# Gate rows summed in the norm transitions, modulation units as halves of wider ones, and VectorE's order changed at three places

## The reference, cut to what matters

```python
mod_lat = jnp.split(jax.nn.silu(c) @ w_ada[l] + b_ada[l], 6, axis=-1)       # first block
x = x + gt2[:, None, :] * swiglu(modulate(rmsnorm(x, g_ffn[l]), sh2, sc2), w_ffn_in[l], w_ffn_out[l])

(sh1, sc1, g1, sh2, sc2, g2, sh3, sc3, g3) = jnp.split(c_act @ w_ada[l] + b_ada[l], 9, axis=-1)  # second
x = x + 0.5 * g1[:, None, :] * swiglu_2(modulate_2(rmsnorm_2(x, ffn1_norm[l]), sh1, sc1), ...)
x = x + g2[:, None, :] * (merged @ w_out[l])        # merged: two gated attention branches
x = x + 0.5 * g3[:, None, :] * swiglu_2(modulate_2(rmsnorm_2(x, ffn2_norm[l]), sh3, sc3), ...)

def swiglu_2(h, w_in, w_out):
    g, u = jnp.split(h @ w_in, 2, axis=-1)          # w_in: 1024 x 5632, w_out: 2816 x 1024
    return (jax.nn.silu(g) * u) @ w_out
```

## Time and profile before

| what | value |
|---|---|
| three runs | 1147.42 us median (1146.41 to 1147.8) |
| the profiled execution | 1146.86 us, of which the span of its instructions is 1145.1 us |
| mean granted TensorE clock | 0.992 |
| TensorE busy | 97% of the span |
| VectorE busy | 75% |
| ScalarE busy | 50% |
| HBM traffic | 218 GB/s over the span |

### The profile page before, as it was taken

The page is one execution under the profiler, slowest core; times in us unless marked ns, Lnnn a source line. Parts: engine busy times, 40 slices in busy tenths (PEclk is TensorE's granted clock), DMA queues, the critical chain, the costliest instruction groups (busy, mean ns, idle before and its releaser), DMA issues.

```text
span 1145.1 us, 19091 instructions
## 1 busy us (share of the span) xinstructions
PE 1107.0 (97%) x7728; PEld 1000.4 (87%) x7728; DVE 854.3 (75%) x1084; ACT 571.4 (50%) x733; POOL 74.8 (7%) x143
## 2 busy tenths in 40 slices
PE   2999999999999999999999999999999999999996
PEld 2899989999999888888788888889999998888885
DVE  1578795997777787777888877878677877655676
ACT  2495443544433644544554445455655646454442
POOL 4000000100001000000300000021000001000001
PEclk8899999999999999999999999999999999999999
DMA  9934656788866587778378777748865645655771
GB/s 283 302 114 135 196 159 206 215 291 267 288 212 204 173 270 255 256 258 294 107 258 291 233 249 259 234 138 267 281 203 179 229 151 184 202 185 203 233 240 37
DMA packets 192548, 250.29 MB, mean 219 GB/s; under 512 B 4859, under 2 KB 171966, under 8 KB 192350
## 3 DMA queue, kind: packets, MB, share of 16 engines
q1 hardware_dynamic: 183838, 216.92, 58.4%
q0 software_dynamic: 8640, 32.38, 8.6%
HBM read 248.23 MB, written 1.05 MB: 218 GB/s over the span
## 4 chain that ended last, share of the span: by engine, by line
PE 85%; DVE 7%; ACT 2%; SPq 2%; issue 1%; DMA 1%; POOL 0%; POOLq 0%; DVEq 0%; ACTq 0%
PE twin L1303 83%; DVE wlo L1917 2%; DVE arena L1925 2%; DVE arena L1917 1%; ACT arena L877 1%; DMA arena<-in_w_ada 1%; ACT whi L877 1%; DVE X L1917 1%; PE twin L1633 1%; SPq L574 0%; SPq L524 0%; DVE arena L1921 0%; PE twin L1754 0%; PE twin L1428 0%; DVE B_lo L1917 0%
## 5 line engine op out<-in xcount | busy, mean ns | idle before, releaser
L1303 PE MATMUL twin<-A_both,whi 128*128 128x256 f32 (+1 forms) x2208 | 577.4, 338 | 3.1 <-DVE A_both L1917 1.6
L1917 DVE TENSOR_TENSOR wlo<-raw,whi 128x2048 fp32r<-128x2048 f32 (+1 forms) x171 | 387.0, 2264 | 120.3 <-ACT whi L877 120.2
L1303 PE MATMUL twin<-A_both,wlo 128*128 128x256 f32 x1632 | 436.5, 280 | 0.0
L877 ACT ACTIVATE whi<-raw 128x2048 fp32r<-128x2048 f32 x169 | 323.2, 1912 | 198.7 <-PE twin L1303 194.9
L1303 PEld LDWEIGHTS twin<-A_both,whi 128*128 128x128 f32 x2208 | 370.1, 190 | 44.1 <-issue 6.2
L1303 PEld LDWEIGHTS twin<-A_both,wlo 128*128 128x128 f32 x1632 | 309.2, 189 | 11.4 <-DVE A_both L1917 0.6
L1925 DVE SCALAR_TENSOR_TENSOR arena<-ada_raw,arena 128x256 f32<-128x256 f32 (+2 forms) x322 | 167.3, 520 | 16.0 <-issue 1.8
L877 ACT ACTIVATE arena<-twin 128x512 f32<-128x512 f32 (+5 forms) x171 | 90.8, 556 | 116.9 <-PE twin L1303 86.3
L877 ACT ACTIVATE arena<-arena 128x512 f32<-128x512 f32 (+7 forms) x132 | 69.6, 558 | 148.8 <-DVE arena L1917 115.8
L1303 PE MATMUL twin<-whi,B_hi 128*128 128x512 f32 (+2 forms) x340 | 126.6, 372 | 0.2 <-DVE B_lo L1917 0.2
L1303 PE MATMUL twin<-wlo,B_hi 128*128 128x512 f32 (+2 forms) x340 | 125.1, 368 | 0.0
(11 more groups left out here) (137 smaller groups left out, 884.3 us busy)
## 6 DMA issues: line engine op xcount, KB each, us to landing
raw<-in_w_in SPq DMA_DIRECT2D x48, 1024.0 KB, 6.3
raw<-in_ffn_w_in SPq DMA_DIRECT2D x44, 1024.0 KB, 5.1
ada_raw<-in_w_ada POOLq DMA_DIRECT2D x28, 1024.0 KB, 6.3
ada_raw<-in_w_ada SPq DMA_DIRECT2D x24, 1024.0 KB, 5.4
raw<-in_w_ffn_in SPq DMA_DIRECT2D x22, 1024.0 KB, 5.2
raw<-in_ffn_w_out SPq DMA_DIRECT2D x22, 1024.0 KB, 5.0
raw<-in_w_ffn_out SPq DMA_DIRECT2D x11, 1024.0 KB, 5.0
arena<-in_w_ada SPq DMA_DIRECT2D x8, 1024.0 KB, 12.0
```

Source lines behind the costliest of these rows:

```text
L877: return nc.scalar.activation(o, i, f, **kw)
L1303: return nc.tensor.matmul(o, l, r, start=start, stop=stop, **kw)
L1917: return nc.vector.tensor_tensor(o, x, y, op)
```

## The change

Seven edits:

- **Cut of the modulation.** All units are now loaded and accumulated as `adapt_half` was: 512 columns by half of the rows, four VectorE instructions of 128x512 in place of eight of 128x256.
- **Counts.** The first two feed-forward blocks take 12 units each (before 10), the third none (before 4). The units are no longer at one place of each step: `ADA_STEP` = 1, 3, 6, 8, 11, 13, 16, 18, 21, 23, 26, 28, where 3i is the place after `low`, 3i + 1 after `split(u0 + 4)`, and 3i + 2 after `split(u0 + 5)` of step i. SP's queue issues the next unit right after the place of the one before.
- **Steps written out.** VectorE's and SP's steps of the feed-forward blocks are written out in place of a loop; TensorE and ScalarE loop in all three blocks.
- **Gates.** The two matmuls of a gate are split (`gate_half`). For gates 1 to 4 the first stands after the sums of shift and scale in `norm(2)` to `norm(5)`, the second after the transposes, in place of the `keep_warm` there; only `norm(3)` keeps a `keep_warm`, of 8 in place of 16. Gate 0 stands after the transposes of the last `ga` unit. Banks are chosen anew and TensorE gets waits for them (`x_piece`, `x_ready`).
- **Gate rows.** VectorE's `gate_row` of gates 1, 2 and 4 stands at the start of the feed-forward block, ahead of `split(u0 + 2)`, that of gate 3 at the start of the second mixer. TensorE waits for it (`gr_done`) in the middle of the second `up` unit, and ahead of `uq` in the second mixer. The wait for the bias moves from TensorE to VectorE.
- **End of a feed-forward block.** ScalarE's `high` and VectorE's `low` stand ahead of the `split(u0 + 3 * NF)` that they followed.
- **Second mixer.** The `split` of the second `out2` unit followed the first `brb` unit on VectorE, ahead of the low halves of the merged branches; it now follows the second `brb` unit. On ScalarE it follows the high halves in place of preceding them.

Constants and banks:

```diff
-NADA1, NADAF, NADA2 = 16, 10, 12
+NADA1, NADAF, NADA2 = 16, 12, 12
 ADA_P2 = NADA1 + 2 * NADAF
-ADA_LAST = ADA_P2 + NADA2
+ADA_STEP = [1 + 5 * j // 2 for j in range(NADAF)]
...
-            return 7 if n in (3, 4) else 3
+            return 7 if n == 4 else 0
...
-            return {0: 6, 3: 2}.get(r, 4)
+            return ((2, 3), (3, 4), (7, 3), (1, 3), (3, 5))[r][x]
```

SP's queue:

```diff
-                def step(i, m):
...
+                def next_ada(q):
+
+                    if f < 2 and q in ADA_STEP[:-1]:
+                        load_ada(NADA1 + NADAF * f + ADA_STEP.index(q) + 1)
+
+                def step(i):
+                    cs = slice(UC * i + UC, UC * i + 2 * UC)
+                    load(u0 + 2, i, w_in[:, :, cs], KD)
+                    next_ada(3 * i - 4)
+                    load(u0 + 3, i, w_in[:, :, DFF + UC * i + UC:DFF + UC * i + 2 * UC], KD)
+                    next_ada(3 * i - 3)
+                    load(u0 + 4, i, w_out[:, 2 * i:2 * i + 2, :], 2)
+                    if f < 2 and i == 0:
+                        load_ada(NADA1 + NADAF * f)
+                    next_ada(3 * i - 2)
```

ScalarE:

```diff
                 silu(NF - 1, u0, 4)
+                high(NF - 1, NF - 1)
                 split(u0 + 3 * NF)
-                high(NF - 1, NF - 1)
                 split(u0 + 3 * NF + 1)
...
                 for n2 in range(N2):
-                    if P2[n2 - 1] == ("brb", 0):
-                        split(BASE_P2 + n2 + 2)
                     if n2:
                         evac2(n2 - 1)
-                    if P2[n2 - 1] != ("brb", 0):
-                        split(BASE_P2 + n2 + 2)
+                    split(BASE_P2 + n2 + 2)
```

TensorE:

```diff
             def norm(n):
                 src = norm_source(n)
+                r = n - 1
+                if n == 3:
+                    pe.wait_ge(x_piece, 1)
                 shift_and_scale(n, column_bank(n))
-                warm = {2: 4, 5: 5}.get(n, 3)
+                if n == 4:
+                    pe.wait_ge(x_piece, 6)
+                gate_half(r, 0)
+                if n == 3:
+                    keep_warm(6, 8)
                 for t in range(TT):
-                    if t == 0:
-                        keep_warm(7 if n in (2, 5) else 6, {2: 4, 3: 16}.get(n, 5))
-                    else:
+                    if t:
                         turn_sums(n, column_bank(n))
...
-                keep_warm(warm, 3)
...
+                if n in (3, 4):
+                    pe.wait_ge(x_piece, 4 * (n - 2))
+                else:
+                    pe.wait_ge(x_ready, 1 if n == 2 else 5)
+                gate_half(r, 1)
...
                     for half in range(2):
+                        if half and gates:
+                            pe.wait_ge(gr_done, gates)
...
-                up(u0 + 1, 0, 2)
+                up(u0 + 1, 0, 2, (2, 3, 5)[f])
...
                 pe.wait_ge(prod_done, n0 + NF)
-                gate((1, 2, 4)[f])
                 down(u0 + 2, NF - 1, NF - 1, False, True)
...
-                    if (kind, n) == ("out2", 0):
-                        gate(3)
...
-                if kind == "mix_out" and n == 0:
-                    gate(0)
...
+                    if n == 3:
+                        gate_half(0, 0)
+                        gate_half(0, 1)
```

VectorE:

```diff
-            def adapt_half(n):
-
-                m, h = n - n % 2, n % 2
+            def adapt(n):
+
+                m, h, g = n - n % 2, n % 2, 2 * ADA[n][0]
...
                 def step(i, m):
                     product(i, 4 if m else 0)
                     split(u0 + 3, i)
                     low(i, m)
+                    adapt_after(3 * i)
                     split(u0 + 4, i)
...
+                    adapt_after(3 * i + 1)
                     split(u0 + 5, i)
-
+                    adapt_after(3 * i + 2)
+
+                gate_row((1, 2, 4)[f])
                 split(u0 + 2)
                 step(0, 0)
-                feed_forward_steps(dve, f, step)
+                for i in range(1, NF - 1):
+                    step(i, i)
                 product(NF - 1, 4)
+                low(NF - 1, NF - 1)
                 split(u0 + 3 * NF)
-                low(NF - 1, NF - 1)
-                r = (1, 2, 4)[f]
-                gate_row(r)
-                dve.wait_ge(gr_done, r + 1)
+                dve.wait_ge(gr_done, (2, 3, 5)[f])
...
                         if n == 0:
-                            split(BASE_P2 + n2 + 3)
                             merged_low(0)
                             merged_low(1)
...
+                    if P2[n2 - 1] == ("brb", 1):
+                        split(BASE_P2 + n2 + 1)
```

More of the change, by code:

```diff
@@ L467, in lin, with feed_forward_steps @@
             return a * i + b
-        def feed_forward_steps(eng, f, step):
-            end = NF - 1 if f < 2 else NF - 4
-            with eng.Fori(0, (end - 1) // 3) as j:
+        def feed_forward_steps(eng, step):
+            with eng.Fori(0, (NF - 2) // 3) as j:
                 for m in range(1, 4):
                     step((j, m), m)
-            for i in range(end, NF - 1):
-                step(i, i)
         def cview(w, c0, n=UC):
@@ L858, in _ @@
                 root(rs2[:, 2 * j:2 * j + 2], ss2[:, 2 * j:2 * j + 2], w).then_inc(lat_rs, 1)
-            for n in range(ADA_P2, ADA_LAST):
+            for n in range(ADA_P2, len(ADA)):
                 if n > ADA_P2:
```

102 lines of the change are left out of this document (33 added, 69 removed).

## The result

The changed kernel takes 1138.59 us (median of four runs, 1138.17 to 1139.3) where the kernel before takes 1147.61 beside it: a ratio of 0.9924, 95% interval 0.9912 to 0.9936. That is 9.0 us less between the medians, 0.76% by the ratio; the forecast was 1140.1 us. Timed again with five runs on another occasion it took 1138.51 against 1146.64, a ratio of 0.9927 (0.9914 to 0.9941).

What follows compares the result with a forecast made beforehand. TensorE, busy for 97% of the span, was taken as the bound, with gains only at seams: 1.55 + 1.55 + 1.71 + 1.6 + 0.9 = 7.3 us, so a median of 1140.1 us, with 8 in 10 from 1138.2 to 1143.8.

Steps and rivals of the forecast that it cites:

- Ends of the blocks: Gates 1, 2 and 4 leave the stretch ahead of the last `down`: 1.55, 1.55 and 1.71 us gained.
- Step 0 to 1: Shorter or no modulation unit ahead of `split(u0 + 5)` removes TensorE's 0.53 us stall: 1.6 us for three blocks.
- The later steps: Modulation units at places 3i + 2 of blocks 1 and 2: zero cost, 0.4 us of slack; upper bound 2.4 to 4.8.
- the rival of late VectorE: VectorE becomes late at the eight tight places, 0.5 us each, 4 us in all: 1141 to 1144 us, chance 0.13.
- Gate 3: Gate moved from ahead of `out2` in the second mixer: 0.9 us gained, 0.8 of 1.7 becoming a new wait.
- The first mixer: Faster modulation in the first mixer gives nothing, as nobody waits for it.
- the low half at the edge: `gla_out` units in the first mixer move towards VectorE's last low half: zero, with a bound of -0.7 us.
- the zero for gate 0: Gate 0 stays inside the first mixer, moves by some units and costs the same.
- The end: First gate multiply of block 3 to the end of the kernel: forecast gain 0.
- The clock: Rival: TensorE's clock falls in `norm(3)` from idling and transposes: 1142 to 1144.5 us, chance 0.10.
- Slower by fetching: Rival: fetching written-out steps makes VectorE late in each step; at 0.5 us each 1153.6 us; slower has chance 0.03.
- nothing shifts: Rival: something else sets the transitions; only step 0 and gate 3 stalls are won: 1145 to 1147, chance 0.07.

Runs made afterwards that it cites:

- e1: Changed kernel with gates of the three feed-forward blocks back ahead of the last `down`, their rows ahead of the gate multiplies: 1143.87 us.
- e9: Changed kernel with two second-mixer splits earlier, GpSimd's turning copies one split earlier in block 2, ScalarE's end-of-block split ahead of `high` again: 1136.99 us.
- e2: Changed kernel with ScalarE's and VectorE's split for the next stage ahead of `high` and `low` again at block ends: 1140.07 us.
- e4: Changed kernel with one extra unused VectorE multiply behind the modulation unit at place 1 of block 1 and places 8, 11, 23, 26 of block 2: 1141.38 us.
- e6: Changed kernel with the first mixer's modulation in the old units of eight 128x256 instructions: 1140.21 us.
- e10: Changed kernel with four `keep_warm` multiplies in place of eight in the transition to block 2: 1139.54 us in one run.
- e5: Changed kernel without the eight `keep_warm` multiplies of the transition to block 2: 1140.65 us.
- e12: Changed kernel with steps 1 to 9 of block 3 as a loop again on VectorE and SP: 1139.55 us in one run.

## Why the prediction was right, point by point

- *Ends of the blocks, 1.55, 1.55 and 1.71 us.* Shown by e1: 1.63, 1.65 and 1.74. That VectorE's split sets the multiply in blocks 1 and 2 stands in the row at 552.30, and e9, where the multiply waits for TensorE, gains only 0.1 us more at each of the two ends. The sentence that the moved `low` "is what makes this possible" was too strong: e2 puts it at 0.5 and 0.4 us. The prediction did not see that the gate rows on VectorE would have held the multiply as well, so that, by the rows of e1, moving them was as needed as moving the gates.
- *Step 0 to 1, 0.53 us in each of three blocks.* The stall went in all three, and 0.1 us more each: step 1 itself had taken 16.75, 16.74 and 16.70 us before and takes 16.63, since a late product also delays what follows it. e4 shows that the unit's length was the cause in block 1.
- *The later steps, nothing.* Right in block 1 within 0.12 us. In block 2 the cover was 0.22 us thinner at places 8 and 23, and the four steps lost 0.54 us between them. The failed term is the 3.0 us for the four instructions. From their start to the next instruction they take 3.23 us in block 1 (427.34 to 430.57) and 3.44 in block 2 (620.22 to 623.66), since the prediction took 0.75 us for each with nothing between them, and did not ask what runs beside them on GpSimd. The 0.4 us of slack, with 0.15 of signalling in it, was otherwise right: the 0.23 us more of block 1 just used it up, and the 0.44 more of block 2 put the next product 0.18 us back. This is the rival of late VectorE, at a seventh of its price.
- *Gate 3, 0.9 us.* 0.86 at `out2`, with a new wait of 0.67 in place of 0.8. Another 0.12 went in the mixer's first 90 us, which was not tried further.
- *The first mixer, nothing.* It gave 0.30 us. "Nobody waits for it" was wrong in both directions: e6 shows stalls in both halves that hang on the length of the units, one of them the low half at the edge. With the old units the second half of the mixer, which holds this edge, takes 0.45 us more (e6), within the stated bound of 0.7; so the zero for gate 0 came true with the help of a part that the prediction gave no effect.
- *The end, nothing.* It gave 0.68 us. Not in the prediction at all.
- *The clock.* It held in nine profiles with 1.35 us of idling and in the one of e10 with 2.26; in the one of e5, with 3.13, it fell. The prediction's 4.4 us from the last matmul to the fall was one of fourteen values that go from 2.05 to 4.95, so it was no firm ground for either side. Its price for a fall, 2.2 to 4.3 us, was one and a half to three times the 1.4 us measured. Of the slow 6.8 us the first 0.9 were idling and only the last 0.7 fell on the products of block 2. Between them lay the transposes and half a gate, which took 5.24 us in place of 4.20 and not twice as long, since at full speed TensorE idles for 0.7 us among them. By the rule of the Trainium skill ("TensorE: Matmul & The Clock Gate", "Part 4: PE-mode transpose") this rival should have come true. The traces decide otherwise for this length: 4.3 us in the changed kernel and 5.3 in e10 passed between ordinary matmuls with idling and transposes alone, at 1.00, though behind the last matmul the clock also fell after as little as 2.05 us. In e5 transposes did not bring the clock back either: it returned only behind ordinary matmuls, which agrees with the rule.
- *Slower by fetching, and "nothing shifts".* Both are refuted, by e12 and by e1.

So 7.3 us were forecast and 7.9 came. The misses of minus 0.46 in block 2 and plus 0.98 in two places outside the argument partly cancel, and that much of the close total is luck. For the two profiled executions the forecast was 1139.5 and the time 1138.17 us: 0.6 of the 1.4 us between them are the stretches, the rest is the start, which was 0.77 us shorter in the profile of the changed kernel than in that of before. The medians, 1140.1 against 1138.6, lie as far apart, but how much of that is the start is not shown.

## What to carry to other kernels

When work is moved to another slot of a periodic schedule, list what every other engine does in that slot, and in which memory both have their operands; a slot that was free on VectorE was taken on GpSimd, and the offset of a wait that looked arbitrary had kept the two apart. When two engines hold the same instruction, removing one holder gives little, by the rows of e1: look for both before counting the gain. And cut two executions at common marks before comparing them. Here the stretches repeat to about 0.1 us, while the start alone moves a single execution by up to 1.5.

## What the hardware showed that I had not expected

- An 8 KB instruction transfer among the last stores took 0.53 to 0.63 us and went with an end that is 0.68 us longer: in both profiles of the kernel before, and in none of the other twelve. That the transfer is the cause was not tried by itself.
- VectorE's 128x512 multiply-and-add with both large inputs in SBUF takes 0.97 us in place of 0.74 beside a 128x256 copy on GpSimd, and the copy 1.06 in place of 0.67. Beside a 128x2048 split the copy takes 2.61, as if it waited for the split's end.
- The granted clock of TensorE fell 2.2 us behind the last matmul ahead of an idle stretch (e5: still 1.00 in the 561st microsecond, 0.84 in the 562nd), and between 2.05 and 4.95 us behind the last matmul of the kernel in fourteen profiles that hardly differ there. What sets the delay of one execution stays open.
